# Hybrid encoder step on one NeuronCore: x arrives in halves of its columns, the first unit starts on the first half, and the norm's sums of squares move into the second unit

## The reference

```python
x = x + 0.5 * SwiGLU_1(RMSNorm(x))
h = RMSNorm(x); p = h @ W_in
y_A = sigmoid(o) * GroupNorm(mLSTM(q, k, v, i, f))
y_B = silu(g) * GroupNorm(Retention(rope(q), rope(k), v))
x = x + concat(y_A, y_B) @ W_out
x = x + 0.5 * SwiGLU_2(RMSNorm(x))
# then a last RMSNorm; states C, n, m and R are outputs too

def rms_norm(x, g):
    y = x * rsqrt(mean(x * x, axis=-1) + EPS)
    return y * g
```

## Time and profile before

| | |
|---|---|
| median of 3 runs | 1074.53 us (1074.39 to 1075.54) |
| the profiled execution | 1074.62 us |
| its span | 1072.9 us |
| mean granted TensorE clock | 0.997 of full speed |
| TensorE busy | 1057.4 us (99% of the span), 8428 matmuls |
| VectorE busy | 689.7 us (64%) |
| ScalarE busy | 465.1 us (43%) |
| GpSimd busy | 220.3 us (21%) |

### The profile page before, as it was taken

How to read it: one execution, slowest core, us unless ns; L and a number is a source line. 1 busy time by engine, 2 the same in 40 slices (tenths; PEclk the granted TensorE clock), 3 DMA queues, 4 the chain that set the end, 5 groups by cost and what they waited for, 6 DMA issues and landing times.

```text
span 1072.9 us, 20465 instructions
## 1 busy us (share of the span) xinstructions
PE 1057.4 (99%) x8428; PEld 1052.9 (98%) x8428; DVE 689.7 (64%) x1142; ACT 465.1 (43%) x813; POOL 220.3 (21%) x182
## 2 busy tenths in 40 slices
PE   7999999999999999999999999999999999999997
PEld 6999999999999999999999999999999999999997
DVE  6987752357866676555655556598875235877544
ACT  7466641246662245333322223446664124666323
POOL 2442100022201220210332222244310002220111
PEclk9999999999999999999999999999999999999998
DMA  7489572388833366445454225547958337983322
GB/s 223 90 184 199 108 184 87 101 162 173 174 85 97 63 129 122 70 57 75 74 78 69 72 65 73 139 89 169 205 109 186 90 92 155 180 179 63 109 72 84
DMA packets 245061, 127.00 MB, mean 118 GB/s; under 512 B 9088, under 2 KB 243624, under 8 KB 244840
## 3 DMA queue, kind: packets, MB, share of 16 engines
q1 hardware_dynamic: 206952, 106.81, 41.2%
q0 software_dynamic: 38016, 18.88, 14.3%
HBM read 122.38 MB, written 3.28 MB: 117 GB/s over the span
## 4 chain that ended last, share of the span: by engine, by line
PE 97%; ACT 1%; DMA 1%; DVE 0%; SPq 0%; issue 0%; POOL 0%; ACTq 0%
PE dense L565 55%; PE dense L664 30%; PE core_banks L664 5%; PE core_banks L800 1%; PE core_banks L815 1%; PE core_banks L818 1%; PE core_banks L790 1%; PE core_banks L565 1%; PE dense L714 1%; DMA x_tok<-in_x_prompt 1%; PE core_banks L784 0%; PE core_banks L827 0%; PE core_banks L786 0%; PE core_banks L701 0%; PE core_banks L601 0%
## 5 line engine op out<-in xcount | busy, mean ns | idle before, releaser
L1293 DVE TENSOR_TENSOR w_lo<-w_raw,w_hi 128x1024 fp32r<-128x1024 f32 (+2 forms) x119 | 131.6, 1124 | 55.4 <-ACT w_hi L945 55.3
L565 PE MATMUL dense<-xg_hi,w_hi 128*128 128x272 f32 x768 | 162.5, 293 | 1.7 <-DVE xg_lo L1298 1.7
L565 PE MATMUL dense<-xg_lo,w_hi 128*128 128x272 f32 x768 | 158.8, 288 | 0.0
L565 PE MATMUL dense<-xg_hi,w_lo 128*128 128x272 f32 x768 | 158.8, 288 | 0.0
L945 ACT ACTIVATE w_hi<-w_raw 128x1024 fp32r<-128x1024 f32 (+2 forms) x120 | 107.2, 907 | 96.3 <-PE dense L565 82.4
L565 PE MATMUL dense<-h_hi,w_hi 128*128 128x272 f32 x684 | 142.5, 290 | 0.0
L565 PE MATMUL dense<-h_lo,w_hi 128*128 128x272 f32 x684 | 141.3, 288 | 0.0
L565 PE MATMUL dense<-h_hi,w_lo 128*128 128x272 f32 x684 | 141.1, 287 | 0.0
L664 PE MATMUL dense<-x_op_hi,w_lo 128*128 128x272 f32 x432 | 124.8, 289 | 0.0
L664 PE MATMUL dense<-x_op_hi,w_hi 128*128 128x272 f32 x432 | 124.8, 289 | 0.0
L664 PE MATMUL dense<-x_late_hi,w_hi 128*128 128x272 f32 x432 | 124.7, 289 | 0.0
(11 more groups left out here) (299 smaller groups left out, 2146.5 us busy)
## 6 DMA issues: line engine op xcount, KB each, us to landing
w_src<-in_w_ffn_gate SPq DMA_DIRECT2D x90, 256.0 KB, 4.5
w_raw<-in_w_ffn_up SPq DMA_DIRECT2D x90, 256.0 KB, 3.6
w_raw<-in_w_in SPq DMA_DIRECT2D x32, 512.0 KB, 8.4
w_raw<-in_w_ffn_down SPq DMA_DIRECT2D x32, 384.0 KB, 3.9
w_raw<-in_w_ffn_down SPq DMA_DIRECT2D x32, 320.0 KB, 3.5
w_src<-in_w_ffn_gate POOLq DMA_DIRECT2D x36, 256.0 KB, 5.7
w_raw<-in_w_ffn_up POOLq DMA_DIRECT2D x36, 256.0 KB, 5.6
w_raw<-in_w_ffn_gate SPq DMA_DIRECT2D x8, 512.0 KB, 5.7
```

What stands on the lines that cost most here:

```text
L565: last = nc.tensor.matmul(out[:, half, 0:TH], w[:, s % 4, k, :], x(kt)[:, half * TH:(half + 1) * TH], start=start and n == 0 and m == 0, s ...
L1293: nc.vector.tensor_tensor(w_lo[:, s % 4, 0:nk, :], w_raw[:, s % RAW, 0:nk, :], w_hi[:, s % 4, 0:nk, :].bitcast(F32), ALU.subtract).then_in ...
```

## The change

x is loaded in halves of its 1024 columns: first the left halves of all five chunks, then the left half (4 k-tiles) of the first weight tile, then the right halves, then the rest of the weight tile and the second weight tile. Only the gain of the first norm is loaded at the start, by ScalarE's queue; the other gains come later and are turned in unit 2. TensorE turns the five left pieces, waits, turns the first right piece, and then starts unit 0, with the other four right pieces turned between its k-tiles 0 to 3. Two right pieces are copied to `xT` by ScalarE instead of VectorE. The first weight tile is split in two halves. The squares of the left halves stay at the start; those of the right halves, and both of the sample chunk, come after weight tile 1 is split, four on ScalarE and two on VectorE. GpSimd adds the two half sums of a chunk before it spreads them. The norm sums move from behind k-tile 4 of unit 0 to behind k-tile 3 of unit 1. Weight tiles 2 and 3 are both split before the root.

```diff
-    X_ORDER = (0, 1, NC, 2, 3)
-    X_PIECES = [(c, half) for c in X_ORDER for half in ((0, 1) if c < NC else (0,))]
+    LEFT, RIGHT = range(2)
+    X_LANDS = [(c, LEFT) for c in range(NC + 1)] + [(c, RIGHT) for c in (0, 1, NC, 2, 3)]
+    X_MOVED = {piece: n + 1 for n, piece in enumerate(X_LANDS)}
+    X_BY_ACT = ((2, RIGHT), (3, RIGHT))
+    X_BY_DVE = [piece for piece in X_LANDS if piece not in X_BY_ACT]
+    X_TAKEN = {piece: n + 1 for n, piece in enumerate(X_BY_DVE)}
+    SQUARES_ACT = [(c, LEFT) for c in range(NC)] + [(NC, LEFT), (NC, RIGHT), (0, RIGHT), (2, RIGHT)]
+    SQUARES_DVE = [(1, RIGHT), (3, RIGHT)]
+    X_COLS = [slice(0, D // 2), slice(D // 2, D)]
...
-        gain_rows = sb("gain_rows", [5 * DT, P])
-        x_squared = sb("x_squared", [P, D])
-        x_sums = sb("x_sums", [P, NC + 1])
+        gain_first = sb("gain_first", [DT, P])
+        x_squared = sb("x_squared", [P, 2, NC + 1, D // 2])
+        x_sums = sb("x_sums", [P, 2, NC + 1])
+        x_total = sb("x_total", [P, NC + 1])
...
+        def x_bank(c, half):
+            if c == NC:
+                return dense[1][:, 1, half * P:(half + 1) * P]
+            return X[:, c, :] if c < 3 else dense[1][:, 0, :]
+        def x_piece(c, half):
+            tiles = x_bank(c, half).rearrange("p (k d) -> p k d", k=DT // 2)
+            return xT[:, half * DT // 2:(half + 1) * DT // 2, CH[c]], tiles
...
+            for c, half in X_LANDS[:NC + 1]:
+                load_x(c, half)
+            sp.dma_start(w_raw[:, 0, 0:DT // 2, :], w_rows(w_ffn1_gate)[:, 0:DT // 2, 0:P]).then_inc(half_loaded, 16)
+            for c, half in X_LANDS[NC + 1:]:
+                load_x(c, half)
+            sp.dma_start(w_raw[:, 0, DT // 2:DT, :], w_rows(w_ffn1_gate)[:, DT // 2:DT, 0:P]).then_inc(w_loaded[0], 16)
+            sp.dma_start(w_raw[:, 1, :, :], w_rows(w_ffn1_up)[:, :, 0:P]).then_inc(w_loaded[1], 16)
+            for n, g in enumerate((g_mix, g_ffn2)):
...
-                    pe.wait_ge(x_taken, len(X_PIECES) - 2 * (1 - t))
                     return
...
+                    if n == 0 and u == 0:
+                        first_unit()
+                        continue
                     pe.wait_ge(w_lo_ready, s + 1)
                     tile_free(t)
-                    if u == 0:
+                    if n == 0 and u == 1:
+                        product(s, bank_of(t), *xg, range(SUMS_K[0]), True, False)
+                        norm_sums_of(0)
+                        product(s, bank_of(t), *xg, range(SUMS_K[0], DT), False, True).then_inc(unit_done, 1)
+                    elif n == 0 and u == 2:
+                        pe.wait_ge(gains_loaded, 16 * 5)
+                        nc.tensor.transpose(X[:, 3, DT:5 * DT], gain_rows[:, :], ident[0:4 * DT, 0:4 * DT]).then_inc(gains_moved, 1)
+                        product(s, bank_of(t), *xg, range(DT), True, True).then_inc(unit_done, 1)
+                    elif u == 0:
                         product(s, bank_of(t), *xg, range(SUMS_K[norm]), True, False, ready=xg_ready(norm))
-                        if n:
-                            pe.wait_ge(y_ready, 2 * H)
+                        pe.wait_ge(y_ready, 2 * H)
                         norm_sums_of(norm)
...
+            def turn_x(c, half):
+                pe.wait_ge(x_loaded[c][half], 16)
+                if half == RIGHT:
+                    pe.wait_ge(x_taken, X_TAKEN[(c, LEFT)])
+                r = P if c < NC else TS
+                for k in range(DT // 2):
+                    j = half * DT // 2 + k
+                    last = nc.tensor.transpose(x_bank(c, half)[:, k * r:(k + 1) * r], x_tok[0:r, c, j * P:(j + 1) * P], ident[0:r, 0:r])
+                last.then_inc(x_moved, 1)
+            def first_unit():
+                pieces = iter(X_LANDS)
+                for _ in range(NC + 1):
+                    turn_x(*next(pieces))
+                pe.wait_ge(gains_ready, 1)
+                for _ in range(KEEP_WARM):
+                    nc.tensor.transpose(X[:, 3, 0:P], x_tok[:, 0, 0:P], ident[:, :])
+                turn_x(*next(pieces))
+                pe.wait_ge(half_lo, 1)
+                for kt in range(DT):
+                    if kt == DT // 2:
+                        pe.wait_ge(w_lo_ready, 1)
+                    last = product(0, bank_of(0), *xg, [kt], kt == 0, kt == DT - 1, ready=xg_ready(0))
+                    for _ in range((1, 2, 1, 0, 0, 0, 0, 0)[kt]):
+                        turn_x(*next(pieces))
+                last.then_inc(unit_done, 1)
...
             def plain(n, norm):
                 for u in range(2 * STD):
                     s, t, j = U_STD[n] + u, T_STD[n] + u, u // 2
-                    if u + 2 < 2 * STD:
+                    if n == 0 and u == 0:
                         split_hi(0, s + 2, 0)
+                        split_hi(0, s + 3, 0)
+                    elif u + 2 < 2 * STD and (n or u > 1):
+                        split_hi(0, s + 2, 0)
+                    if n == 0 and u == 2:
+                        act.wait_ge(gains_moved, 2)
+                        nc.scalar.activation(gains[:, DT:5 * DT], X[:, 3, DT:5 * DT], ACT.Copy).then_inc(gains_ready, 1)
...
+            def square_x(c, half):
+                act.wait_ge(x_loaded[c][half], 16)
+                r = P if c < NC else TS
+                nc.scalar.activation(x_squared[0:r, half, c, :], x_tok[0:r, c, X_COLS[half]], ACT.Square,
+                                     accum_out=x_sums[0:r, half, c:c + 1]).then_inc(x_summed, 1)
+            nc.scalar.dma_start(gain_first[:, :], g_ffn1[0].rearrange("(k p) -> k p", p=P)).then_inc(first_gains_loaded, 16)
             act.wait_ge(consts_ready, 2)
             link(nc.scalar.activation(unused[:, :], eps[:, :], ACT.Square))
-            for n, c in enumerate(X_ORDER):
-                act.wait_ge(x_loaded[c], 16)
-                if c == NC - 1:
-                    act.wait_ge(x_end_loaded, 16)
-                if n:
-                    act.wait_ge(x_summed, n)
-                r = P if c < NC else TS
-                nc.scalar.activation(x_squared[0:r, :], x_tok[0:r, c, :], ACT.Square, accum_out=x_sums[0:r, c:c + 1])\
-                    .then_inc(x_summed, 1)
-                if c == 2:
-                    split_hi(0, 0, 0)
-            act.wait_ge(gains_moved, 1)
-            nc.scalar.activation(gains[:, :], X[:, 3, 0:5 * DT], ACT.Copy).then_inc(gains_ready, 1)
-            for j in range(DT):
-                act.wait_ge(x_taken, len(X_PIECES) - (j < DT // 2))
+            for c in range(NC):
+                square_x(c, LEFT)
+                if c == 0:
+                    act.wait_ge(gains_moved, 1)
+                    nc.scalar.activation(gains[:, 0:DT], X[:, 3, 0:DT], ACT.Copy).then_inc(gains_ready, 1)
+            act.wait_ge(half_loaded, 16)
+            nc.scalar.activation(w_hi[:, 0, 0:DT // 2, :], w_raw[:, 0, 0:DT // 2, :], ACT.Copy).then_inc(half_hi, 1)
+            act.wait_ge(x_taken, NC + 1)
+            for j in range(DT // 2):
+                normed_hi(0, j, None, G_FFN1, 0)
+            for piece in X_BY_ACT:
+                act.wait_ge(x_moved, X_MOVED[piece])
+                out, tiles = x_piece(*piece)
+                nc.scalar.activation(out, tiles, ACT.Copy).then_inc(x_taken_act, 1)
+            act.wait_ge(w_loaded[0], 16)
+            nc.scalar.activation(w_hi[:, 0, DT // 2:DT, :], w_raw[:, 0, DT // 2:DT, :], ACT.Copy).then_inc(w_hi_ready, 1)
+            act.wait_ge(x_taken, len(X_BY_DVE))
+            act.wait_ge(x_taken_act, len(X_BY_ACT))
+            for j in range(DT // 2, DT):
                 normed_hi(0, j, None, G_FFN1, 0)
             split_hi(0, 1, 0)
+            for c, half in SQUARES_ACT[NC:]:
+                square_x(c, half)
...
+            def take_x(piece):
+                dve.wait_ge(x_moved, X_MOVED[piece])
+                out, tiles = x_piece(*piece)
+                nc.vector.tensor_copy(out, tiles).then_inc(x_taken, 1)
+            for piece in X_BY_DVE[:NC + 1]:
+                take_x(piece)
+            normed_lo(0, 0, 0, G_FFN1, 0)
+            normed_lo(0, 1, 0, G_FFN1, 0)
+            take_x((0, RIGHT))
+            normed_lo(0, 2, 0, G_FFN1, 0)
+            take_x((1, RIGHT))
+            take_x((NC, RIGHT))
+            for j in range(3, DT):
                 normed_lo(0, j, 0, G_FFN1, 0)
             dve.wait_ge(w_lo_ready, 1)
             split_lo(0, 1, 0)
+            for c, half in SQUARES_DVE:
+                x = x_tok[:, c, X_COLS[half]]
+                nc.vector.tensor_tensor_reduce(x_squared[:, half, c, :], x, x, 1.0, 0.0, ALU.mult, ALU.add,
+                                               x_sums[:, half, c:c + 1]).then_inc(x_summed_dve, 1)
...
-            for n, c in enumerate(X_ORDER):
+            pool.wait_ge(half_hi, 1)
+            nc.gpsimd.tensor_tensor(w_lo[:, 0, 0:DT // 2, :], w_raw[:, 0, 0:DT // 2, :], w_hi[:, 0, 0:DT // 2, :].bitcast(F32),
+                                    ALU.subtract).then_inc(half_lo, 1)
```

(32 more changed lines are left out.)

70 lines of the change are left out of this document (20 added, 50 removed).

## The result

The changed kernel takes 1083.11 us (median, 1082.09 to 1083.91); the kernel before, run beside it, 1074.38 us (1074.33 to 1075.54). The ratio is 1.0078, with a 95% interval of 1.0065 to 1.009: slower by 8.7 us, where 4.1 were forecast. The profiled execution took 1082.82 us with a span of 1081.1, 8.2 more than before's.

The account below looks back on a forecast made before the run. TensorE, busy in 99% of the span, was taken as the bound, with only unit 2's start counting. Unit 2 at 32.1 instead of 27.96 us adds 4.1 to 1074.6: 1078.7 us, range 1075.3 to 1082.5.

Parts of the forecast that it names:

- What bounds the kernel, and that only unit 2's start counts: TensorE is busy in 99% of the span; the change is worth what it does to unit 2's start at 27.96 us.
- Unit 0 starts earlier: At the start, x's left halves let unit 0 begin at about 9.9 us instead of 14.74, a gain of 4.8 us.
- Unit 0 is fed more slowly: Right pieces and weight halves delay unit 0's second half; unit 1 starts at 20.0 to 20.7 us instead of 21.93.
- what would show it: Signs in the profile after: TensorE's longest wait behind the start on the eviction or GpSimd's spreads, eviction ending about 32 us.
- The norm is late: Sums inside unit 1, even on time, delay unit 0's eviction, so unit 2 starts 1.2 to 1.8 us later.
- the most that the change could bring: With the norm chain hidden altogether, unit 2 starts 0.3 to 1.0 us before 27.96: 1073.6 to 1074.3 us.
- GpSimd is later still: GpSimd's additions and spreads take 4.75 us plus 1.1 for blocking by VectorE; sums end at 25.9, unit 2 starts at 32.1.
- The full blocking rival: VectorE and GpSimd alternate through GpSimd's whole list of additions and spreads: +6.8 us, 1081.4 us; chance 22%.
- The clock: Rival: TensorE's clock falls behind its stops ahead of unit 2, losing 1.8 us: 1080.5 us; chance 15%.
- Behind unit 2: After unit 2's start nothing is counted; everything runs back to back and is not touched by the change.

Follow-up runs that it names:

- before_halves: The kernel before, with x's first four chunks each loaded as two transfers of half the columns, in the same order; 1075.52 us, ratio 1.0008.
- warm_first: The changed kernel with 22 transposes that nobody reads ahead of k-tile 4 of unit 0; 1083.24 us, ratio 1.0083 to the kernel before.
- sums_after_unit0: squares_in_gap with the norm's sums ahead of unit 1's products instead of four k-tiles into them; 1077.94 us, ratio 1.0029 to the kernel before.
- squares_in_gap: The changed kernel with right-half squares in ScalarE's and VectorE's idle time and three spreads ahead of GpSimd's second half weight tile; 1079.78 us.
- quiet_dve: The changed kernel, with VectorE waiting for all five spreads of the sums before it splits weight tiles 2 and 3; 1080.62 us, ratio 1.0059.
- warm_both: warm_first with 30 more transposes that nobody reads ahead of the norm sums; 1082.01 us, ratio 1.0071 to the kernel before.
- x_first: The kernel before, with all x in whole rows first, then the first weight tile in halves, gains last, its low halves on VectorE; 1075.0 us.

## Why the prediction was wrong in size

The direction and the chain held: unit 2 waits for unit 0's eviction, that for the norm's sums, and these for GpSimd. The size did not: 4.1 us were forecast and 8.7 measured, and 1083.1 us lies above the range of 1075.3 to 1082.5. Four terms of the sum were too small: x's left halves in `xT` (+1.2 us), TensorE's time to the last right piece (+0.6 net), GpSimd's list with its blocking (+1.2), and the sums on TensorE (+1.07), where the price of a slower clock was left to a rival. Each step is set against its own figure, from one stage to the next:

| step | forecast | measured | off |
|---|---|---|---|
| unit 0 starts | 9.9 | 11.07 | +1.2 |
| from there to hi part 4 | 5.2 | 5.8 | +0.6 |
| from there to GpSimd's first addition | 4.9 | 4.9 | 0 |
| GpSimd's list | 5.9 | 7.05 | +1.2 |
| sums on TensorE | 0.92 | 1.99 | +1.07 |
| handovers, root, reciprocal, eviction, gains' transpose, unit 2 | 5.3 | 5.4 | +0.1 |

But for roundings they add up to the difference of 4.1, the 36.23 us of the trace against 32.1.

**What bounds the kernel, and that only unit 2's start counts:** right. Both kernels have the same 1044.9 us behind it.

**Unit 0 starts earlier:** right in kind, 3.7 us for the 4.8 forecast. The first transposes came at 3.73 us (forecast 3.5), but the five left pieces were in `xT` at 9.3 and not at 8.1 us. I took the pace of the first transposes for the arrival of the pieces, and the rate of whole rows from the earlier trace rows for half rows. ScalarE's squares of successive left halves show the arrivals:

```profile
3.77 0.63 ACT L1200 ACTIVATE x_squared<-x_tok 128x512 f32<-128x512 f32 x1 [0.85 <-DMA x_tok<-in_x_prompt]
...
4.97 0.63 ACT L1200 ACTIVATE x_squared<-x_tok 128x512 f32<-128x512 f32 x1 [0.42 <-DMA x_tok<-in_x_prompt]
...
6.40 0.63 ACT L1200 ACTIVATE x_squared<-x_tok 128x512 f32<-128x512 f32 x1 [0.70 <-DMA x_tok<-in_x_prompt]
```

They are 1.2 to 1.4 us apart, where 262 KB at the rate of before take 0.7. before_halves puts about 1.0 us on half rows in the kernel before. That the 1.2 us here are the same effect is likely, not shown: no run has the changed kernel with whole rows.

**Unit 0 is fed more slowly:** right, and understated. TensorE took 4.8 us from its first product to the last right piece, where I had 3.8. My terms give 4.1 if they are added up correctly. The first k-tile still ran at the slow start rate, 1.28 us (11.07 to 12.35) where I had 0.75; in the kernel before, TensorE was past that rate when unit 0 began. The copy and the split cost a little less than I had (1.05 for 1.4 us), GpSimd's half what it should (1.27 us, forecast 1.2 to 1.3). Unit 1 started at 23.61 us, not 20.0 to 20.7. What of this lies ahead of hi part 4 reached unit 2 through ScalarE and GpSimd. Of the rest, warm_first shows that the clock's 1.3 us did not. The stop ahead of k-tile 4 was foreseen (2.5 us), but it is the longest behind the start, not one on the eviction or the spreads, as I wrote under what would show it.

**The norm is late:** shown. sums_after_unit0 takes 1.8 us off squares_in_gap by moving the sums alone, and in squares_in_gap TensorE waits 2.19 us for the eviction though the sums came on time. The forecast of 1.2 to 1.8 us for this part is of the same size, though it was counted from an earlier unit 1. That unit 1 was late too is what I missed in the most that the change could bring. I had put unit 2 at 27.0 to 27.7 us with the norm hidden; in sums_after_unit0, where it is hidden, unit 2 starts at 32.1.

**GpSimd is later still:** the place was right; its price is the step that failed most, and the one that was weighed and not only read off. An addition takes 0.18 us (I took 0.25, the upper bound), and left alone the list would be about 4.1 us: four pairs of 0.86 us by quiet_dve's rows, and a smaller one for the sample. It took 7.05, so 2.9 us were blocking, where the full price was 3.7 and I had taken 1.1. That the list alone is shorter than my 4.75 us hid 0.65 of the miss. I chose a third because one spread in the kernel before had not stretched the lo part beside it. That row was weak evidence: the spread ran from 13.38 to 13.99 us and the lo part began at 13.81, so at most 0.18 us could have shown, and it showed VectorE's side only. The Trainium skill (SBUF — State Buffer, section "SBUF: two separate sides") has the two engines lock each other out of a shared port. Here GpSimd's rows agree: up to 1.1 us more on a 0.60 us spread. VectorE pays too when GpSimd is first: in quiet_dve its first two lo parts, behind the start of GpSimd's half weight tile, took 1.95 us for 1.48. The full blocking rival had the better size here.

**The clock:** I gave it 15% and 1.8 us. The granted clock did fall behind both stops, but ahead of unit 1 it cost nothing (warm_first). At the sums 1.07 us were lost (0.92 to 1.99): at the full clock the sums behind a wait still took 1.18 us (quiet_dve, warm_both), so 0.8 are the clock's, and 0.26 come with starting behind a wait. The medians put both filled stops at about 1.1 us (warm_both), within the spread of its runs. So this rival was true beside my case and not in place of it; I had priced the cases as if they excluded each other, which is also why the range ended too low. (Its lower end should have been 1075.8, 1074.6 + 1.2, and not 1075.3; that decided nothing.)

**Behind unit 2:** nothing, as forecast, in the profiled execution.

That leaves a budget for the 8.7 us, by medians. All misplacement of squares and spreads together is 3.3 us (squares_in_gap). The blocking by the two splits and the clock at the sums that hangs on it, 2.5 (quiet_dve), are another cut through the same loss and not to be added. The sums' place is 1.8 (sums_after_unit0). The other 3.5 no run took off. The slow first product, the stop of 2.5 us between unit 0's halves and, likely, the half rows lie in them; how they share it is open.

## What to carry to other kernels

Ahead of a stretch that runs without a gap, only the start of that stretch has a value. Here unit 0 started 3.7 us earlier, and it was lost in what came next: the second half of unit 0's feed, and a norm that had 1.4 us of cover. Work that is moved off a busy engine must be set against what its new neighbours do at that moment: the same instructions cost 3.3 us less in an idle stretch two steps earlier. And when several mishaps each follow from the same late stage, add them up in the forecast; they are not alternatives.

## What the runs showed of the hardware

**A stop does not always lower the clock.** After a stop of 2.49 us in sums_after_unit0 the granted clock was 0.64 over the next 24 matmuls; after one of 2.9 us in squares_in_gap it was 1.00. First the one, then the other:

```profile
20.20:24.99 4.79, 4.79 (x25) 4.79 (x26) 4.79 (x6) 4.59 (x5) 3.48 (x3) 0.64 0.44 120
```

```profile
16.46:19.36 2.90, 0.00 (x0) 0.03 (x1) 1.85 (x2) 2.90 (x6) 2.71 (x5) 1.00 0.57 110
19.36:22.60 3.24, 3.24 (x24) 3.04 (x24) 3.24 (x5) 3.22 (x5) 3.14 (x3) 1.00 0.59 167
```

The Trainium skill (TensorE: Matmul & The Clock Gate, section "The HAM clock gate") says that idle time brings half rate back. Of the nine stops of over 2 us behind the start in the changed kernel and its five variants, five agree: behind 2.11 and 2.48 us in the changed kernel, 2.48 in quiet_dve, 2.49 in sums_after_unit0 and 3.39 in warm_first the granted clock of the first two or three us behind the stop was 0.50 to 0.56. Behind 2.19 us in warm_both it fell only 0.9 us after unit 2's start. Behind 2.46 us in quiet_dve, and behind 2.2 and 2.9 in squares_in_gap, it stayed at 1.00. So the length of the stop alone does not decide it; what does stays open.

**The start has two outcomes.** The times of x_first (11 runs) lie at 1073.5 to 1073.8 (4 runs) and 1075.0 to 1075.4 (7 runs), those of the kernel before at 1074.1 to 1074.8 (16) and 1075.4 to 1076.1 (7). The two transposes' rows above come from one run near each group, and unit 2 starts 1.6 us apart in them, as do the spans (1071.7 and 1073.3). before_halves gives a third: its profiled execution is in the upper of its groups (1076.4 and 1076.6, where the other nine are at 1075.0 to 1075.7), and there TensorE was at the slow rate until about 17.2 us. So the groups are likely set by when TensorE leaves its slow start rate; the granted clock reads 1.00 in all three, and only the durations show it. The kernels differ in other ways too, so this is an inference and not shown.
